# Both loops of a two-layer encoder kernel written out: no loop turns and no register arithmetic on any engine

## The chip, the cores and the metric

The kernel runs on one core of a Trainium2 chip. The metric is device time in microseconds (us) of one execution, from start to end of the program on that core. A core has five engines that matter here, each with a sequencer of its own that reads its own stream of instructions: TensorE (PE, matrix products; PEld is its weight load), VectorE (DVE), ScalarE (ACT), GpSimd (POOL) and SyncE (SP, which here issues all data transfers). They meet only at semaphores.

## The reference: what is computed

Two layers over a sequence of 1024 tokens with 1024 channels, in float32. Each layer modulates its input with a shift and a scale, mixes, multiplies with a gate, and normalises.

```python
for i in range(2):
    mod = silu(c) @ ada_w[i] + ada_b[i]
    shift, scale, gate = split(mod, 3)
    h = x * (1 + scale) + shift
    y = dilated_attention(h) if i == 0 else state_space(h)
    x = layer_norm(alpha * x + gate * y, ln_g[i], ln_b[i])
```

Layer 0 is attention with 16 heads of 64 channels and three dilations (1, 4, 16). For each dilation there are queries, keys and values; a query sees 128 keys around it, with a bias that falls with the distance. The three results are weighed by their softmax denominators, multiplied with silu of a gate projection, and projected.

Layer 1 is a bidirectional state-space mixer with 4 groups of 8 heads: a projection, a convolution over 5 tokens and silu, then for each direction a scan over 8 chunks of 128 tokens. A chunk contributes a masked product inside the chunk and a state of 128 x 512 that is carried, decayed, to the next chunk. The sum of both directions and a skip term is gated, normalised by its root mean square and projected.

## The kernel before

There is one hand-written program for each engine and each layer. Nothing is scheduled by a planner: the order of the work on an engine is the order in which the Python functions are called, and every dependency between engines is a semaphore with a count.

**Attention.** The projections run in units of two tiles (128 output channels each). Every unit is seven products of 12 matmuls (four blocks of the contraction, three terms of a high and a low float32 part), in a Strassen-like scheme: POOL and ACT make the seven weight forms (`low_part` L573 and around, `round_form`), PE multiplies (`product`, L688), DVE adds the seven products up in PSUM (`first_sums`, `second_sums`, L1317 to L1341). Between the units PE does the attention of the current head pair in ten "duos": `scores` (L742), `transpose_probs` (L752), `values` (L810, L821). DVE takes the row extremes (`tops`, L1282) and copies transposed probabilities (`copy_t`, L1302), ACT takes the exponentials (L1048) and copies projections and numerators (L987).

There are eight head pairs. Pairs 0 to 6 run in a loop with a register `j` on each engine; the eighth stands behind the loop as straight code (`last_pair` and its like) and does the same things in its first six duos. The five loops of the five engines are separate: PE's at L939, ACT's at L1177, POOL's at L649, SP's at L478, DVE's at L1537, and each engine turns around at its own place. DVE turns around just before the duo 1 of the next pair, behind the addition of L1330.

**State space.** Groups 0 to 2 run in a loop with a register `j` (PE L2535, ACT L2859, POOL L2296, SP L2173, DVE L3207), group 3 stands behind it as straight code with less and other work. What precedes group 0 is straight code as well. A group has eight chunk steps. In each one PE does six quarters of a projection unit for the next group (`project_k`, L2340), the state of a chunk (`state`, L2357), and `outputs` (L2372 and L2384). ACT opens the group with `conv_weights` (L2584 to `gconv`), the rounding of a weight tile (`split_hi`, L1970, to `w_hi_s`), `shift` (L2653), `back` (L2584 to `vv`), `centre` (L2593, L2595) and `exponentials` (L2660). POOL takes the low part of that tile (`split_lo`, L1960), then the inputs of the state (`decayed_inputs`, L2227, `xw`), and `weights` (L2240). DVE does `convolve` (L2970), `lesser` (L2898), `both` (L2906), `update` (L2917 to L2928). SP loads rows of factors (`load_rows` L2022, `load_ew` L2028) and weight tiles (`load_w` L1948). The last thing that ACT does in a group is `skip` of the fourth tile (L2584 to `trunk`), which waits for a transfer of SP (`send`, L2074) to be finished.

**How a loop is made.** In a loop every count that depends on `j` is worked out in registers by the engine's own sequencer, ahead of the instruction that waits for it, and so is every address that depends on `j` (`bass.ds(j, 1)`). At the end of the body stand an addition and a conditional branch.

```python
with act.Fori(0, GROUPS - 1) as j:
    group(j, False)
group(LAST, True)
```

Some helpers ask `isinstance(n, int)`: it tells a value known in Python (straight code) from a register (loop), and chooses a wait or a buffer by that.

Of the kernel before, what the change touches and what calls it, by code (L numbers as in the profile page):

```python
# [115 lines left out]
def attention_phase(nc, io, keep):  # L116
# [7 lines left out]
    with ExitStack() as ctx:  # L124
# [186 lines left out]
        def programs(block, after):  # L311
# [4 lines left out]
            def _(sp):  # L316
# [161 lines left out]
                with sp.Fori(0, PAIRS - 1) as j:  # L478
# [82 lines left out]
            def _(pool):  # L561
# [87 lines left out]
                with pool.Fori(0, PAIRS - 1) as j:  # L649
# [31 lines left out]
            def _(pe):  # L681
# [257 lines left out]
                with pe.Fori(0, PAIRS - 1) as j:  # L939
                    pair(j)  # L940
# [30 lines left out]
            def _(act):  # L971
# [205 lines left out]
                with act.Fori(0, PAIRS - 1) as j:  # L1177
# [91 lines left out]
            def _(dve):  # L1269
# [267 lines left out]
                with dve.Fori(0, PAIRS - 1) as j:  # L1537
# [172 lines left out]
def state_space_phase(nc, io, keep, first):  # L1710
    with ExitStack() as ctx:
# [131 lines left out]
        def x_place(n, i):  # L1843

            if isinstance(n, int) and i % 2:
                return yo_p[:, 0, :], yo_p[:, 1, 0:P]
            return fill[:], bt_p
# [78 lines left out]
        def paired(n, k):  # L1926

            return int(isinstance(n, int) and n == 0 and 0 < k < 7)
# [34 lines left out]
        def split_hi(act, n, slot):  # L1963
            act.wait_ge(w_in, 16 * n + 16)

            if not isinstance(n, int) or n > 3:
                wait(act, "pp_full", 2 * n - 2)
            elif n > 1:
                wait(act, "pp_full", n + 1)
# [47 lines left out]
        def programs(block):  # L2017
            @block.sync
            def _(sp):
                def load_rows(j, c):  # L2020
                    src = io["cum_rows"][c, :, bass.ds(j, 1)].rearrange("d a h t -> d (a h t)")
# [3 lines left out]
                def load_ew(j, c):  # L2025
                    for half in range(2):
                        src = io["exp_rows"][half, c, :, bass.ds(j, 1)].rearrange("d a k t -> d (a k t)")
# [3 lines left out]
                def load_fac(n):  # L2031
                    sp.dma_start(fac[:], io["fac"][bass.ds(n, 1)].rearrange("a p k -> p (a k)")
# [37 lines left out]
                def send(j, i):  # L2070
                    kt, hf_ = i // 2, i % 2
                    wait(sp, "y_gated", 8 * j + (i + 1))
                    dst = io["yT"][4 * hf_:4 * hf_ + 4, :, bass.ds(4 * j + kt, 1), :]
# [99 lines left out]
                with sp.Fori(0, GROUPS - 1) as j:  # L2173
                    group(j, False)
# [38 lines left out]
            def _(pool):  # L2213
# [82 lines left out]
                with pool.Fori(0, GROUPS - 1) as j:  # L2296
# [40 lines left out]
            def _(pe):  # L2337
# [51 lines left out]
                def unstage(n, i):  # L2389
                    if i == 0:  # L2390
                        wait(pe, "silu_done", UB * n + 10)
                    if not isinstance(n, int):
# [142 lines left out]
                with pe.Fori(0, GROUPS - 1) as j:  # L2535
# [46 lines left out]
            def _(act):  # L2582
# [18 lines left out]
                def tanh(tile, f, banked=False):  # L2601

                    wait(act, "pp_free", 3 if isinstance(tile, int) and tile == 0 else 2 * tile + 2)
# [17 lines left out]
                def conv_weights(g):  # L2621

                    src = conv[:, g, :] if isinstance(g, int) else conv[:, bass.ds(g, 1), :].rearrange(
                        "p a c -> p (a c)")
# [4 lines left out]
                def skip_weights(n):  # L2629
                    put(dg[:], dcol[:, bass.ds(4 * n, 4)]).then_inc(S["dg_set"], 1)  # L2630

                def skip(n, kt):
# [3 lines left out]
                    if not isinstance(n, int):  # L2636
# [222 lines left out]
                with act.Fori(0, GROUPS - 1) as j:  # L2859
# [35 lines left out]
            def _(dve):  # L2895
# [311 lines left out]
                with dve.Fori(0, GROUPS - 1) as j:  # L3207
# [137 lines left out]
```

## Time and profile before

| | |
|---|---|
| time of the kernel, three runs | 2128.47, 2129.84, 2132.52 us, median 2129.84 us |
| the execution that was profiled | 2126.8 us, of which the span of the instructions is 2124.7 us |
| mean granted clock of PE | 0.985 |
| attention loop, turns of the branch taken | 6 on each engine |
| state-space loop, turns of the branch taken | 2 on each engine |
| a pair of the attention loop | about 131 us |
| a group of the state-space loop | about 167 us |

The profile is a page of summaries, and views of the trace by line, by wait, by time, by window, and along the chain of work that ended last. In the views, "q" behind an engine (ACTq) is an instruction of its sequencer: register arithmetic, a branch, a semaphore, a transfer that it issues. "issue" is time in which an engine waited for nothing that the profile shows.

### The profile page before, as it was taken

How to read it: one execution, taken by the hardware profiler on the slowest of the kernel's cores; microseconds unless marked ns; L12 is line 12 of the kernel's file. 1: busy time of each engine (PE TensorE's matmuls, PEld its weight loads, DVE VectorE, ACT ScalarE, POOL GpSimd, SP SyncE). 2: the span in 40 equal slices, each digit the busy share in tenths (PEclk: the TensorE clock that was granted, in tenths of full speed). 3: DMA queues.
4: the chain of work that ended last, by engine and by line, in shares of the span. 5: the costliest groups of instructions: out<-in, count | busy, mean ns of one | idle time of the engine just before them, and what ended most of it. 6: DMA issues, size and time to landing. Idle time of an engine off the chain costs nothing.

```text
span 2124.7 us, 34188 instructions
## 1 busy us (share of the span) xinstructions
PE 1978.9 (93%) x10607; PEld 1569.4 (74%) x10607; DVE 1365.9 (64%) x2731; ACT 1052.8 (50%) x2574; POOL 1276.2 (60%) x845
## 2 busy tenths in 40 slices
PE   2689999999999999999997989899899899998997
PEld 1467777777777777777776868677687677777886
DVE  7745746557475564755646676797497498487553
ACT  3245455455445455544554254773574475584320
POOL 3456686775867758677583345475275366386572
PEclk9999999999999999999999999999999999999998
DMA  7312131221212222122224423464265265377431
GB/s 237 113 60 73 50 91 58 72 72 61 79 58 72 75 66 81 58 72 80 61 79 160 153 100 103 124 185 137 82 182 156 93 168 153 102 195 234 159 119 40
DMA packets 119606, 229.11 MB, mean 108 GB/s; under 512 B 22592, under 2 KB 65216, under 8 KB 119488
## 3 DMA queue, kind: packets, MB, share of 16 engines
q1 hardware_dynamic: 119488, 227.85, 34.7%
q8 instruction: 36, 0.59, 0.1%
q14 instruction: 82, 0.67, 0.1%
HBM read 199.42 MB, written 28.39 MB: 107 GB/s over the span
## 4 chain that ended last, share of the span: by engine, by line
PE 65%; DVE 14%; issue 8%; ACT 4%; POOL 4%; DMA 3%; SPq 1%; DVEq 0%; ACTq 0%; POOLq 0%
PE pp L688 24%; PE po L688 9%; PE pp_s L2340 7%; PE tp L752 3%; PE sp_ L742 3%; PE yo_p L2544 3%; DVE stage_s L2970 2%; DMA w_raw_s<-in_b_w 2%; PE pp_s L2544 2%; PE po L821 2%; DVE vv L2906 2%; PE st_p L2544 1%; PE po L810 1%; PE fill L2544 1%; PE tp L761 1%
## 5 line engine op out<-in xcount | busy, mean ns | idle before, releaser
L688 PE MATMUL pp<-h_forms_hi,w_f 128*128 128x512 f32 x1600 | 529.2, 400 | 42.2 <-DVE h_forms_lo L1438 31.9
L688 PEld LDWEIGHTS pp<-h_forms_hi,w_f 128*128 128x128 f32 x1600 | 304.0, 190 | 111.4 <-issue 42.0
L563 POOL TENSOR_TENSOR w_f<-w_raw,w_f 128x512 fp32r<-128x512 f32 x160 | 206.8, 1311 | 181.1 <-ACT w_f L987 181.1
L688 PE MATMUL pp<-h_forms_lo,w_f 128*128 128x512 f32 x800 | 314.3, 393 | 0.0
L2340 PE MATMUL pp_s<-h_hi,w_hi_s 128*128 128x512 f32 x624 | 270.5, 433 | 16.8 <-DVE stage_s L2970 9.6
L1048 ACT ACTIVATE prob<-prob,mz 128x256 f32<-128x256 f32 (+2 forms) x384 | 170.0, 444 | 231.6 <-DVE mz L1282 231.4
L2340 PE MATMUL pp_s<-h_hi,w_lo_s 128*128 128x512 f32 x624 | 246.3, 395 | 0.0
L2340 PE MATMUL pp_s<-h_lo,w_hi_s 128*128 128x512 f32 x624 | 246.0, 394 | 0.0
L688 PE MATMUL po<-h_forms_hi,w_f 128*128 128x512 f32 x640 | 214.9, 396 | 4.1 <-POOL w_f L563 4.1
L563 POOL TENSOR_TENSOR w_f<-w_f_raw,w_f 128x512 fp32r<-128x512 f32 x120 | 156.2, 1302 | 101.9 <-ACT w_f L987 101.9
L688 PEld LDWEIGHTS pp<-h_forms_lo,w_f 128*128 128x128 f32 x800 | 152.6, 191 | 29.1
L2340 PEld LDWEIGHTS pp_s<-h_hi,w_hi_s 128*128 128x128 f32 x624 | 118.5, 190 | 65.6 <-issue 35.1
L1302 DVE COPY probT<-tp 128x512 f32<-128x512 f32 x160 | 102.8, 683 | 89.2 <-PE tp L752 70.7
L1960 POOL TENSOR_TENSOR w_lo_s<-w_raw_s,w_hi_s 128x1024 fp32r<-128x1024 f32 x40 | 98.8, 2470 | 101.6 <-ACT w_hi_s L1970 101.6
L2970 DVE SCALAR_TENSOR_TENSOR stage_s<-pp_s,gconv,stage_s 128x512 f32<-128x512 f32 (+2 forms) x184 | 137.9, 750 | 20.4 <-ACT stage_s L2595 14.8
L688 PEld LDWEIGHTS po<-h_forms_hi,w_f 128*128 128x128 f32 x640 | 121.9, 190 | 30.9 <-POOL w_f L563 4.5
L2340 PEld LDWEIGHTS pp_s<-h_lo,w_hi_s 128*128 128x128 f32 x624 | 118.8, 190 | 31.0 <-issue 9.4
L2340 PEld LDWEIGHTS pp_s<-h_hi,w_lo_s 128*128 128x128 f32 x624 | 118.4, 190 | 26.5
L987 ACT ACTIVATE w_f<-w_f_raw 128x512 fp32r<-128x512 f32 x120 | 75.5, 630 | 121.7 <-POOL w_f_raw L608 90.4
L1282 DVE CUSTOM_DVE_ANT_0 prob<-sp_,bias,slope 128x256 f32<-128x256 f32 (+2 forms) x384 | 134.1, 405 | 2.1 <-DVE slope L1518 2.1
L2240 POOL TENSOR_TENSOR vv<-rw,vv 128x1024 f32<-128x1024 f32 x32 | 76.5, 2390 | 97.8 <-DVE vv L2906 81.6
L688 PE MATMUL po<-h_forms_lo,w_f 128*128 128x512 f32 x320 | 126.2, 394 | 0.0
(470 smaller groups left out, 4330.3 us busy)
## 6 DMA issues: line engine op xcount, KB each, us to landing
w_raw<-in_a_w SPq DMA_DIRECT2D x80, 512.0 KB, 3.2
rw<-cum_rows SPq DMA_DIRECT2D x32, 1024.0 KB, 6.2
w_raw_s<-in_b_w SPq DMA_DIRECT2D x40, 512.0 KB, 4.3
ew<-exp_rows SPq DMA_DIRECT2D x64, 256.0 KB, 7.2
qk<-merge_rows SPq DMA_DIRECT2D x42, 256.0 KB, 4.1
yT_b<-trunk SPq DMA_DIRECT2D x32, 256.0 KB, 2.3
v<-in_ada_w SPq DMA_DIRECT2D x40, 192.0 KB, 2.5
stage_s<-yT_b SPq DMA_DIRECT2D x15, 512.0 KB, 4.7
```

Source lines behind the costliest of these rows:

```text
L563: return nc.gpsimd.tensor_tensor(out, x, hi.bitcast(F32), ALU.subtract)
L688: last = nc.tensor.matmul(bank, w[:, b], h[:, b], start=b == 0 and t == 0, stop=b == KS - 1 and t == 2)
L742: last = nc.tensor.matmul(sp_[:, h, c:c + w], q[rows, P * n:P * n + P], kT[g][rows, k0:k0 + w], start=True, stop=True)
L987: return nc.scalar.activation(dst, src, ACT.Copy, **kw)
L1048: last = nc.scalar.activation(prob[:, u % 2, c:c + w], prob[:, u % 2, c:c + w], ACT.Exp, scale=-1.0, bias=mz[:, m:m + 1], accum_out=mz[:, ...
L1282: last = nc.vector.tensor_tensor_reduce(out=prob[:, u % 2, c:c + w], in0=sp_[:, u % 2, c:c + w], in1=bias[:, c0:c0 + w], scale=slope[:, h: ...
L1302: nc.vector.tensor_copy(dst, src).then_inc(t_free, 2 if ev[0] == "e" else 1)
L1960: nc.gpsimd.tensor_tensor(flat(w_lo[:, slot]), flat(w_raw[:]), flat(w_hi[:, slot]).bitcast(F32), ALU.subtract).then_inc(S["lo_done"], 1)
L2240: nc.gpsimd.tensor_tensor(flat(vv[:, c % 2]), flat(rw[:, c % 2, 1]), flat(vv[:, c % 2]), ALU.mult).then_inc(S["wx_done"], 1)
L2340: last = nc.tensor.matmul(out, w[:, slot, k, :], of_h(h, k, half), start=(k == 0 and n == 0), stop=(k == KT - 1 and n == 2))
L2544: ins = nc.tensor.matmul(acc(m, half), y, w[:, half * HALF:(half + 1) * HALF], start=(k == 0 and i == 0), stop=(k == KO - 1 and i == 2))
L2970: ins = nc.vector.scalar_tensor_tensor(out, src[:, a - 2 + k - half * HALF:b - 2 + k - half * HALF], w[:, k:k + 1], out, ALU.mult, ALU.add)
```

## The change

Every one of the ten loops becomes a Python loop, so that the program holds seven copies of a pair's code and three copies of a group's, with all counts and addresses as constants. The order of the working instructions on each engine is unchanged, and so are their number, their shapes and what they wait for. Since `j` is now always known in Python, the helpers' tests are put in terms of its value.

```diff
-                with sp.Fori(0, PAIRS - 1) as j:
+                for j in range(PAIRS - 1):
...
-                with pool.Fori(0, PAIRS - 1) as j:
+                for j in range(PAIRS - 1):
...
-                with pe.Fori(0, PAIRS - 1) as j:
+                for j in range(PAIRS - 1):
...
-                with act.Fori(0, PAIRS - 1) as j:
+                for j in range(PAIRS - 1):
...
-                with dve.Fori(0, PAIRS - 1) as j:
+                for j in range(PAIRS - 1):
...
-            if isinstance(n, int) and i % 2:
+            if n == 0 and i % 2:
...
-            if not isinstance(n, int) or n > 3:
+            if n > 3:
...
-                    src = io["cum_rows"][c, :, bass.ds(j, 1)].rearrange("d a h t -> d (a h t)")
+                    src = io["cum_rows"][c, :, j:j + 1].rearrange("d a h t -> d (a h t)")
...
-                    if not isinstance(n, int):
+                    if n:
                         wait(pe, "xu_free", 8 * n + i)
...
-                with sp.Fori(0, GROUPS - 1) as j:
+                for j in range(GROUPS - 1):
                     group(j, False)
                 group(LAST, True)
...
-                    src = conv[:, g, :] if isinstance(g, int) else conv[:, bass.ds(g, 1), :].rearrange(
-                        "p a c -> p (a c)")
+                    src = conv[:, g, :]
```

The loops of POOL, PE, ACT and DVE over the groups change as SP's does.

Three places, in the order in which instructions stand in the program (REGISTER_ALU and the bare ISA rows are register arithmetic).

ACT, end and beginning of the body of the loop over the groups, before; `trunk` is the output that `skip` begins, `gconv` holds the convolution's weights, `w_hi_s` the rounded weight tile, `rw` a chunk's rows:

```order
L2584 ACTIVATE trunk<-stage_s,dg 128x1024 x4
L2859 UNCONDITIONAL_BRANCH
L2859 ISA
L2584 ISA
L2584 ACTIVATE gconv<-conv 128x36
L1901 REGISTER_ALU
L1964 ISA
L1901 ISA
L1970 ACTIVATE w_hi_s<-w_raw_s 128x1024
L2651 ISA
...
L2859 REGISTER_ALU
L2859 COMPARE_AND_BRANCH
```

The same place now, at the entry of the first copy; the later copies read alike:

```order
L2584 ACTIVATE vv<-cbm,fac 128x128 x8
L2659 ACTIVATE rw<-rw,fac 128x128 x8
L2584 ACTIVATE trunk<-stage_s,dg 128x1024 x4
L2584 ACTIVATE gconv<-conv 128x36
L1970 ACTIVATE w_hi_s<-w_raw_s 128x1024
L2652 ACTIVATE rw<-rw,fac 128x128 x8
```

The five working instructions stand in the same order, with nothing between them.

DVE, end of the body of the loop over the pairs, before; `temps` and `pp` hold sums of the products, `probT` transposed probabilities:

```order
L1327 REGISTER_ALU
L1328 TENSOR_TENSOR temps<-pp,temps 128x512
L1329 REGISTER_ALU
L1330 TENSOR_TENSOR temps<-po,temps 128x512
L1537 REGISTER_ALU
L1537 COMPARE_AND_BRANCH
```

The end of the first copy and the beginning of the second, now:

```order
L1323 TENSOR_TENSOR pp<-pp,temps 128x512
L1328 TENSOR_TENSOR temps<-pp,temps 128x512
L1330 TENSOR_TENSOR temps<-po,temps 128x512
L1302 COPY probT<-tp 128x512 x2
L1282 ISA prob,mz<-sp_,bias,slope 128x256
```

The copy to `probT`, to which DVE had to branch back, follows the addition directly.

SP, the last chunk steps of a group of the state-space loop, before; `rw` and `ew` are rows of factors, `w_raw_s` is a weight tile:

```order
L1901 REGISTER_ALU
L2022 ISA
L2022 DMA rw<-cum_rows 128x2x1024
L1901 REGISTER_ALU
L2028 ISA
L2028 DMA ew<-exp_rows 64x2x512
L2028 ISA
L2028 DMA ew<-exp_rows 64x2x512
L1901 REGISTER_ALU
L1948 ISA
L1948 DMA w_raw_s<-in_b_w 128x1024
```

The same place now:

```order
L2022 DMA rw<-cum_rows 128x2x1024
L2028 DMA ew<-exp_rows 64x2x512 x2
L1948 DMA w_raw_s<-in_b_w 128x1024
```

The four transfers are in the same order, and the register arithmetic between them is gone.

## Rows read from the trace of the kernel before

**Rows 1.** The page: busy time of PE, and what was loaded on the instruction queues.

```profile
PE 1978.9 (93%) x10607; PEld 1569.4 (74%) x10607; DVE 1365.9 (64%) x2731; ACT 1052.8 (50%) x2574; POOL 1276.2 (60%) x845
...
q8 instruction: 36, 0.59, 0.1%
q14 instruction: 82, 0.67, 0.1%
```

**Rows 2.** Windows of attention: loop pairs 1 and 6, then the straight eighth; twice.

```profile
core 0: us, PE busy (x) PEld busy (x) DVE busy (x) ACT busy (x) POOL busy (x), PEclk, DMA share, GB/s
261.72:288.11 26.39, 25.68 (x149) 20.27 (x149) 13.47 (x34) 12.58 (x30) 21.19 (x15) 1.00 0.37 102
...
916.38:942.64 26.26, 25.68 (x150) 20.27 (x149) 13.48 (x34) 12.46 (x31) 21.04 (x15) 1.00 0.36 102
1047.23:1073.13 25.90, 25.66 (x150) 20.30 (x149) 13.56 (x34) 12.63 (x30) 20.76 (x14) 1.00 0.36 103
...
288.11:314.05 25.94, 25.94 (x157) 21.08 (x157) 12.43 (x33) 13.55 (x30) 23.10 (x16) 1.00 0.20 67
...
1073.13:1099.09 25.96, 25.96 (x158) 21.09 (x157) 12.45 (x33) 13.75 (x30) 23.50 (x17) 1.00 0.22 70
```

**Rows 3.** The chain, DVE's first turn (start us, us, what).

```profile
273.92 0.07 DVEq L1537
273.99 3.45 issue
277.44 0.07 DVEq L1537
```

**Rows 4.** PEld in time, where the next pair's values begin.

```profile
start us, us, engine line op out<-in xcount [idle before <-releaser]
284.92 0.85 PEld L821 LDWEIGHTS po<-probT,v 128*64 128x64 f32 x16 [1.08 <-ACT num L987]
```

**Rows 5.** Windows of the state space: two chunk steps in groups 0, 1 and 2.

```profile
1361.34:1387.89 26.55, 24.75 (x142) 19.54 (x141) 23.45 (x39) 22.87 (x70) 17.49 (x10) 1.00 0.60 175
1520.05:1554.82 34.77, 27.74 (x140) 21.00 (x140) 22.68 (x39) 25.13 (x75) 17.79 (x10) 0.85 0.42 132
1686.84:1721.73 34.89, 27.63 (x141) 21.03 (x141) 22.66 (x38) 25.13 (x75) 17.80 (x10) 0.85 0.44 130
1387.89:1449.40 61.51, 59.71 (x341) 47.73 (x340) 57.97 (x100) 42.75 (x126) 45.27 (x27) 1.00 0.58 161
1554.82:1616.29 61.47, 59.72 (x341) 47.73 (x340) 57.99 (x100) 42.90 (x126) 45.28 (x27) 1.00 0.59 161
```

**Rows 6.** ACT in time, its first turn from group 0 to group 1.

```profile
1518.66 1.15 ACT L2584 ACTIVATE trunk<-stage_s,dg 128x1024 f32<-128x1024 f32 x1 [1.10 <-DMA yT_b<-trunk]
1521.54 0.23 ACT L2584 ACTIVATE gconv<-conv 128x36 f32 x1 [1.73 <-issue]
1526.10 1.06 ACT L1970 ACTIVATE w_hi_s<-w_raw_s 128x1024 fp32r<-128x1024 f32 x1 [4.32 <-issue]
```

**Rows 7.** ACT in time, entry into group 0.

```profile
1355.60 3.22 ACT L2584 ACTIVATE trunk<-stage_s,dg 128x1024 f32<-128x1024 f32 x3
1358.73 0.21 ACT L2584 ACTIVATE gconv<-conv 128x36 f32 x1
1359.16 1.06 ACT L1970 ACTIVATE w_hi_s<-w_raw_s 128x1024 fp32r<-128x1024 f32 x1 [0.22 <-ACT gconv L2584]
```

**Rows 8.** POOL in time behind that turn, then PE in time.

```profile
1527.23 2.35 POOL L1960 TENSOR_TENSOR w_lo_s<-w_raw_s,w_hi_s 128x1024 fp32r<-128x1024 f32 x1 [7.24 <-ACT w_hi_s L1970]
1529.54 2.11 POOL L2227 TENSOR_TENSOR xw<-trunk,fac 128x512 f32<-128x512 f32 x1
...
1526.42 0.39 PE L2340 MATMUL pp_s<-h_hi,w_lo_s 128*128 128x512 f32 x1
1531.78 2.07 PE L2357 MATMUL st_p<-xw,bt 128*128 128x512 f32 x2 [4.97 <-POOL xw L2227]
1535.91 0.79 PE L2340 MATMUL pp_s<-h_hi,w_hi_s 128*128 128x512 f32 x1 [2.06 <-DVE stage_s L2970]
```

**Rows 9.** The chain at ACT's turn: the branch, and what follows it.

```profile
1518.74 0.04 ACTq L2859
1518.79 2.55 issue
1521.34 0.07 ACTq L2859
```

**Rows 10.** Window with the lower clock behind ACT's first turn.

```profile
1529.60:1539.80 10.20, 5.96 (x11) 3.62 (x12) 8.77 (x17) 10.20 (x35) 3.81 (x2) 0.50 0.15 51
```

**Rows 11.** Chain, end of a group: SP's queue between POOL and a weight tile; PE.

```profile
1616.28 0.02 issue
...
1618.72 8.40 DMA w_raw_s<-in_b_w
...
1635.05 0.49 PE L2340 MATMUL pp_s<-h_hi,w_hi_s 128*128 128x512 f32 x1 [1.44 <-DVE trunk L3151]
```

**Rows 12.** SP in time, the same transfers in group 3, which is straight code.

```profile
1863.14 0.37 SPq L2022 DMA_DIRECT2D rw<-cum_rows  x1
1863.56 1.32 SPq L2028 DMA_DIRECT2D ew<-exp_rows  x2
1864.92 0.78 SPq L2152 DMA_DIRECT2D hb<-hb_s  x1
```

**Rows 13.** The queues of stretches 100:255 and 260:1040: packets, MB, share of 16 engines.

```profile
q8 instruction: 7, 0.11, 0.3%
q14 instruction: 7, 0.06, 0.1%
...
q14 instruction: 31, 0.25, 0.1%
```

More of the change, by code:

```diff
@@ L1926, in paired @@
         def paired(n, k):
-            return int(isinstance(n, int) and n == 0 and 0 < k < 7)
+            return int(n == 0 and 0 < k < 7)
         def xw_of(n, k):
@@ L2026, in load_ew @@
                     for half in range(2):
-                        src = io["exp_rows"][half, c, :, bass.ds(j, 1)].rearrange("d a k t -> d (a k t)")
+                        src = io["exp_rows"][half, c, :, j:j + 1].rearrange("d a k t -> d (a k t)")
                         sp.dma_start(ew[HD * half:HD * half + HD, c % 2],
@@ L2031, in load_fac @@
                 def load_fac(n):
-                    sp.dma_start(fac[:], io["fac"][bass.ds(n, 1)].rearrange("a p k -> p (a k)")
+                    sp.dma_start(fac[:], io["fac"][n:n + 1].rearrange("a p k -> p (a k)")
                                  ).then_inc(fac_in, 16)
@@ L2072, in send @@
                     wait(sp, "y_gated", 8 * j + (i + 1))
-                    dst = io["yT"][4 * hf_:4 * hf_ + 4, :, bass.ds(4 * j + kt, 1), :]
+                    dst = io["yT"][4 * hf_:4 * hf_ + 4, :, 4 * j + kt:4 * j + kt + 1, :]
                     sp.dma_start(dst.rearrange("m p a t -> p m (a t)"),
@@ L2295, in group @@
                     weights(j + 1, 0)
-                with pool.Fori(0, GROUPS - 1) as j:
+                for j in range(GROUPS - 1):
                     group(j, False)
@@ L2534, in group @@
                             products(j + 1, i // 4)
-                with pe.Fori(0, GROUPS - 1) as j:
+                for j in range(GROUPS - 1):
                     group(j, False)
@@ L2601, in tanh @@
                 def tanh(tile, f, banked=False):
-                    wait(act, "pp_free", 3 if isinstance(tile, int) and tile == 0 else 2 * tile + 2)
+                    wait(act, "pp_free", 3 if tile == 0 else 2 * tile + 2)
                     wait(act, "silu_done", 2 * tile)
@@ L2629, in skip_weights @@
                 def skip_weights(n):
-                    put(dg[:], dcol[:, bass.ds(4 * n, 4)]).then_inc(S["dg_set"], 1)
+                    put(dg[:], dcol[:, 4 * n:4 * n + 4]).then_inc(S["dg_set"], 1)
                 def skip(n, kt):
@@ L2635, in skip @@
                     wait(act, "silu_done", UB * n + (2 * kt + 2))
-                    if not isinstance(n, int):
+                    if n:
                         act.wait_ge(y_out[kt], 32 * n)
@@ L2857, in _ @@
                 SQ_READ = [n + 1 if c == 0 else m + 1 for n, (m, c) in enumerate(ORDER)]
-                with act.Fori(0, GROUPS - 1) as j:
+                for j in range(GROUPS - 1):
                     group(j, False)
@@ L3205, in normalise @@
                                             ALU.mult).then_inc(normed, 1)
-                with dve.Fori(0, GROUPS - 1) as j:
+                for j in range(GROUPS - 1):
                     group(j, False)
```

## The prediction

> **What bounds the kernel now.** I read the page first: PE is busy for 1978.9 of 2124.7 us [rows 1], so almost everything that saves time must let PE start something sooner. DVE, ACT and POOL are busy for 64, 50 and 60% and matter only where PE waits for them. Then I looked for places where a loop's body can be set beside straight code that does the same work, since the change turns the one into the other. Windows of both loops give that [rows 2, 5]. Last I followed the chain and the engines in time around each turn of a loop [rows 3, 4, 6 to 9], the clock behind it [rows 10], the queue of SP [rows 11, 12] and the queues that carry instructions [rows 13].
>
> **Register arithmetic on PE: nothing.** The change takes some thousand register instructions from PE's sequencer. Does PE wait for them? The stretch from duo 2 to duo 4 lasts 25.94 us inside the loop and 25.96 us in the eighth pair, which is straight code with constants [rows 2]. PE is busy throughout in both. So this part is costed at 0. The cover is PE's own work: the arithmetic is done while matmuls are queued, and the equal windows show that it suffices.
>
> **Turns of the attention loop: 2.7 us.** There are six taken turns on each engine. On DVE the branch is followed by 3.45 us in which nothing runs and nothing is waited for [rows 3]. That delays the row extremes of the next duo, then ACT's exponentials and copies, and some ten microseconds later PE stands 1.08 us before the values of the next duo [rows 4]. The window that holds this, duo 0 to duo 2, shows the price: 26.39 us at the first turn, 26.26 at the sixth (26.46, 26.35, 26.36 and 26.24 at those between), against 25.90 in the straight pair, at the same PE busy time of 25.7 [rows 2]. The differences are 0.49, 0.56, 0.45, 0.46, 0.34 and 0.36, together 2.66 us. Most of DVE's 3.45 us is hidden by PE's queue of matmuls. The lower end is 6 x 0.2 = 1.2 us, if a part of the difference is due to the eighth pair's other tiles; the upper end is PE's whole wait, 6 x 1.08 = 6.5 us. I take 2.7, since the window measures PE itself. The turns of the other engines in this loop show no wait on PE and count nothing.
>
> **Turns of the state-space loop: 16.2 us.** Two turns are taken. ACT finishes `skip`, starts `gconv` 1.73 us after it could and the rounding of the weight tile 4.32 us after `gconv`, with no releaser for either [rows 6]. From the start of the last `skip` to the rounding it is 1526.10 - 1518.66 = 7.44 us. At the entry to group 0, which has no turn, the last of the three merged `skip`s starts about 1.05 us before `gconv` at 1358.73, and the rounding comes at 1359.16: 1.48 us [rows 7]. So ACT loses 5.96 us at each turn. Who waits for that: POOL sat 7.24 us before the low part of this tile, and only behind that does it make `xw`; PE waits 4.97 us for `xw`, then 2.06 us for DVE's convolution, which hangs on ACT through the rows [rows 8]. Without the loss POOL ends `xw` at 1531.65 - 5.96 = 1525.7, before PE is through with its matmuls at 1526.65, so the first wait goes. The second wait ends 5.96 us sooner, at 1529.95 in place of 1535.91. PE would reach it about 1.1 us after 1526.65, so 2.2 us of waiting stay there: DVE and ACT are late next. There is a second gain. After the turn PE's granted clock is 0.50, its level of 1.2 GHz, for 10.2 us [rows 10], behind PE's wait of 4.97 us. In the 3.9 us of that stretch in which products run, a matmul of 512 columns takes 0.43 us where it takes 0.23 us elsewhere: ten of them lose 2.0 us. A wait of 2.2 us may or may not lower the clock; group 0 has one of 1.8 us at the same granted clock of 1.00, so I count the 2.0 as gained. Sum of this working: 5.96 + 2.0 = 8.0 us a turn.
>
> The windows give the same in another way. Two chunk steps last 34.77 and 34.89 us behind the turns and 26.55 us in group 0, which is entered without one; the five steps that follow last 61.51 and 61.47 us, alike [rows 5]. The differences are 8.22 and 8.34 us. I take 8.1 a turn, 16.2 for both. Lower end: PE's first wait alone, 4.97 us each, 9.9 in all. Upper end: both waits and the clock, 4.97 + 2.06 + 2.0, 18.1 in all.
>
> **Register arithmetic on the other engines: 1.5 us.** Inside the five equal steps PE is idle for 61.5 - 59.7 = 1.8 us [rows 5], and nothing says that arithmetic is the cause; I take 0, at most 3 x 1.8 = 5.4. At the end of a group a weight tile is late: from POOL's end at 1616.28 to the start of its transfer at 1618.72 SP spends 2.44 us on three other transfers and the arithmetic before each, and the tile's rounding delays what PE waits 1.44 us for [rows 11]. In straight code the same three take 1864.92 - 1863.14 = 1.78 us [rows 12], and I add 0.15 for the waits: 0.5 us sooner, in three groups, 1.5 us. Lower end 0, upper end 3 x 1.44 = 4.3 us.
>
> **Streaming of instructions: 0.** What is added is code to be fetched. Queue 8 carries 36 blocks of instructions in the whole span [rows 1], none in the 780 us of attention loop after its first pass, and 7 in the 155 us around and in that first pass [rows 13]. At that rate, 7 in 155 us, the loops' later passes (790 us of attention, 360 of state space) need about 52 blocks more. PE's price for them is read from straight code: the eighth pair fetches its code, and its steps are as long as the loop's [rows 2]. On the other queue the loops already fetch, 31 blocks in those 780 us [rows 13], so little is added. I take 0; a gain is excluded, the loss is a rival below.
>
> **What the Trainium skill says.** The trace shows 2.55 us between ACT's branch and its next instruction, while the branch itself is 0.04 us [rows 9]. The Trainium skill, "Runtime: NRT & Kernel Launch", section on instruction fetch mechanics, says that fetching is sequential and that a taken branch out of the pages held forces a fetch before the engine can go on; the trace agrees for ACT and DVE. It also says that crossing into a next page of straight code is mostly hidden, which the equal windows bear out.
>
> **The sum.** 2.7 + 16.2 + 1.5 = 20.4 us, from the profiled 2126.8 us: 2106.4 us. That execution was 3.04 us faster than the median of 2129.84 us, so on the median I predict **2109.4 us**, 0.96% less.
>
> **The rivals.** *Half of it in the state space.* ACT's delay goes, but another link takes its place: DVE turns around at the same time, and POOL has three things to do before PE's second wait ends. Then only PE's first wait goes (9.9 us), with 1.2 to 2.7 from attention: 11 to 13 us, about 2118 us. Against it, group 0 has all these links and takes 26.55 us. *More than that.* The arithmetic also holds up the chain between DVE, ACT, POOL and SP inside a group: with the upper ends 6.5 + 18.1 + 4.3 + 5.4 it is 34 us, about 2096; half of the excess gives 2102. For it, the chain has a lot of "issue" in the state space; against it, PE is 97% busy in the equal steps. *The turns cost only the branch.* What follows a branch would have been a wait for something else. The branch of 0.04 us [rows 9] on the deciding engine, eight times, is 0.3 us, and the time stays at 2129.5 us. Against it, the entry to group 0 runs the same instructions without the delay [rows 7].
>
> The "Advanced Engine Details and Errata" page of the Trainium skill, section on control flow timing, gives about 108 ns for a compare-and-branch; by that figure eight turns would be an estimate of 0.9 us, and the time would not measurably change. The trace shows 0.04 us for the instruction, and 2.55 us until the next.
>
> *Slower: PE's code arrives late.* PE's loops now run without fetching. If each of the 52 added blocks held PE up, by as much as a branch holds ACT (2.55 us), the loss would be 133 us; the gain of 20.4 us is used up at 0.4 us a block, and from there the kernel is slower. With 1 us a block it is 2109.4 + 52 = 2161 us. It would be likeliest in the state space, where transfers are busy for 0.58 of the time [rows 5]. Against it stand the windows of the straight pair.
>
> **How the numbers follow.** The forecast, about 2109, has 0.62. Half of it, about 2118, has 0.17. More, about 2100, has 0.12. The turns cost only the branch: 0.05. Slower: 0.04. The range is to leave out no more than the last two and the farthest parts of "more": 2101 to 2119. About 0.2%, 4 us, is what a measurement of this kernel can tell from no change. Faster by more than that is the first three cases, 0.91; no change 0.05; slower 0.04.
>
> **What would show it.** In the profile after: DVE's copy to `probT` follows its addition without the 3.45 us; the windows from duo 0 to duo 2 last 25.9 us in all pairs; ACT's rounding starts about 1.5 us after the last `skip`; the windows of two chunk steps last about 26.6 us in all three groups, at a granted clock of 1.00; queue 8 has some 85 to 90 blocks instead of 36, without a PE wait at them. The prediction is wrong if the two chunk steps stay above 30 us, or if PE shows new idle time of about a microsecond every twenty.

## The result, and the profile after

The straight kernel takes 2112.07 us (median of 4 runs, 2110.16 to 2117.66) against 2129.15 us beside it (2127.25 to 2132.52): a ratio of 0.9919, 95% interval 0.9902 to 0.9936. That is 17 us faster; predicted were 20.4 us and 2109.4. A second comparison gave 2113.77 against 2130.31, ratio 0.9923 (0.991 to 0.9937). The first profiled execution of the straight kernel took 2117.66 us (span 2115.8), 5.6 above its median, while that of before, 2126.8, lay 2.3 below its own. So the two traces differ by 8.9 us only, and below I use a second profile of the straight kernel too (run e10, span 2114.0, 10.7 us below before).

The page of after, the rows that answer to [rows 1]. As predicted, queue 8 carries 50 blocks more; queue 14 carries fewer, since the loops had fetched their bodies again at every turn.

```profile
PE 1976.5 (93%) x10607; PEld 1570.4 (74%) x10607; DVE 1369.5 (65%) x2731; ACT 1054.0 (50%) x2574; POOL 1278.1 (60%) x845
q8 instruction: 86, 1.41, 0.3%
q14 instruction: 63, 0.52, 0.1%
```

Three stretches by windows: up to the state space, its groups 0 to 2, the rest. First before, then after (columns as in [rows 2]). In this pair of executions the whole gain is in the second stretch, 11.4 us, and the attention part gained nothing. The second profile says the same: 1364.7, 477.5 and 271.8 us, so 15.1 us less in the groups and 3.4 us more in what precedes them. What the medians gain beyond that, some 6 us, stands in no trace.

```profile
0.00:1361.34 1361.34, 1268.70 (x6999) 1006.08 (x6999) 841.00 (x1823) 652.09 (x1551) 850.66 (x584) 0.99 0.28 88
1361.34:1853.87 492.53, 463.13 (x2407) 363.22 (x2407) 358.26 (x684) 291.59 (x784) 264.66 (x157) 0.98 0.48 140
1853.87:2124.70 270.83, 247.10 (x1202) 200.16 (x1202) 166.62 (x224) 109.15 (x242) 160.86 (x106) 0.97 0.47 151
```

```profile
0.00:1363.05 1363.05, 1268.89 (x7000) 1006.90 (x7000) 843.36 (x1823) 653.67 (x1552) 851.09 (x584) 0.99 0.29 88
1363.05:1844.16 481.11, 459.90 (x2407) 362.48 (x2407) 359.58 (x684) 291.28 (x784) 264.71 (x157) 0.99 0.50 143
1844.16:2115.80 271.64, 247.74 (x1202) 201.06 (x1202) 166.59 (x224) 109.09 (x241) 162.28 (x106) 0.97 0.47 150
```

Windows of attention after, duo 0 to duo 2 in pairs 1, 2, 5, 6 and the eighth, as in [rows 2]. Pairs 2, 3, 4 and the eighth take 25.7 us, even less than the 25.9 that I expected. Pairs 1, 5 and 6 take longer than inside the loop (26.39, 26.24 and 26.26): something new waits there.

```profile
262.52:290.73 28.21, 25.73 (x151) 20.30 (x150) 15.87 (x34) 12.65 (x30) 21.79 (x15) 1.00 0.35 93
395.32:421.05 25.73, 25.49 (x151) 20.31 (x150) 13.39 (x34) 12.68 (x30) 20.57 (x15) 1.00 0.38 103
...
786.22:812.76 26.54, 25.70 (x151) 20.30 (x150) 14.21 (x34) 12.67 (x30) 20.87 (x15) 1.00 0.36 100
917.32:944.16 26.84, 25.69 (x151) 20.30 (x150) 14.57 (x33) 12.76 (x30) 21.51 (x15) 1.00 0.34 99
1048.72:1074.45 25.73, 25.49 (x152) 20.31 (x150) 13.39 (x34) 12.68 (x30) 20.57 (x15) 1.00 0.38 102
```

Windows of the state space after, two chunk steps in groups 0, 1 and 2, as in [rows 5]. The 34.8 and 34.9 us of groups 1 and 2 are 28.9 and 27.3, the clock is back at 0.94 to 1.00. Group 0 has lost 1.3 us in this execution, at a clock of 0.94; in the second profile it takes 26.3 us at 1.00, so that loss does not belong to the code.

```profile
1363.05:1390.89 27.84, 26.06 (x141) 20.72 (x140) 24.87 (x41) 22.60 (x69) 17.42 (x10) 0.94 0.65 186
1522.05:1550.90 28.85, 26.36 (x140) 20.66 (x141) 23.98 (x41) 23.59 (x72) 17.50 (x10) 0.94 0.58 180
1683.98:1711.24 27.26, 24.77 (x140) 19.51 (x141) 22.59 (x39) 23.61 (x72) 17.51 (x10) 1.00 0.59 170
```

ACT in time at the same place as [rows 6]. Behind the last `skip` the rounding of the weight tile starts after 1.30 us instead of 7.44, with no idle time at all.

```profile
1519.30 1.15 ACT L2584 ACTIVATE trunk<-stage_s,dg 128x1024 f32<-128x1024 f32 x1
1520.35 0.22 ACT L2584 ACTIVATE gconv<-conv 128x36 f32<-128x36 f32 x1
1520.60 1.06 ACT L1970 ACTIVATE w_hi_s<-w_raw_s 128x1024 fp32r<-128x1024 f32 x1
```

### The profile page after: what moved, and what is told of

It is laid out like the page before. It is cut to its first block, busy times and chain, and to the rows that moved or that the text cites. A ratio compares the mean times of both kernels' runs of the same rounds, so it can differ in the third digit from the quotient of the medians.

```text
span 2115.8 us, 30206 instructions
## 1 busy us (share of the span) xinstructions
PE 1976.5 (93%) x10607; PEld 1570.4 (74%) x10607; DVE 1369.5 (65%) x2731; ACT 1054.0 (50%) x2574; POOL 1278.1 (60%) x845
## 4 chain that ended last, share of the span: by engine, by line
PE 67%; DVE 9%; POOL 8%; issue 7%; ACT 5%; DMA 3%; SPq 1%; POOLq 0%; DVEq 0%; ACTq 0%
PE pp L688 25%; PE po L688 9%; PE pp_s L2340 7%; PE tp L752 4%; PE sp_ L742 4%; PE yo_p L2544 3%; DMA w_raw_s<-in_b_w 3%; PE po L821 2%; POOL trunk L2249 2%; PE pp_s L2544 2%; POOL vv L2240 2%; PE po L810 2%; PE st_p L2544 1%; PE fill L2544 1%; POOL w_lo_s L1960 1%
## 5 line engine op out<-in xcount | busy, mean ns | idle before, releaser
L2969 DVE SCALAR_TENSOR_TENSOR stage_s<-pp_s,gconv,stage_s 128x512 f32<-128x512 f32 (+2 forms) x184 | 137.9, 750 | 20.6 <-ACT stage_s L2595 15.1
L2340 PEld LDWEIGHTS pp_s<-h_lo,w_hi_s 128*128 128x128 f32 x624 | 118.6, 190 | 30.9 <-issue 9.4
L2340 PEld LDWEIGHTS pp_s<-h_hi,w_lo_s 128*128 128x128 f32 x624 | 118.1, 189 | 26.6
```

What stands on the lines that cost most here:

```text
L2340: last = nc.tensor.matmul(out, w[:, slot, k, :], of_h(h, k, half), start=(k == 0 and n == 0), stop=(k == KT - 1 and n == 2))
L2969: ins = nc.vector.scalar_tensor_tensor(out, src[:, a - 2 + k - half * HALF:b - 2 + k - half * HALF], w[:, k:k + 1], out, ALU.mult, ALU.add)
```

## The experiments

In all kernels the loops are made by one generator, so that each engine and each loop can be chosen alone: `for j in turns(act, GROUPS - 1, how)`. With nothing said an engine keeps its loop. "Windows" are those of the two chunk steps of groups 1 and 2 (before: 34.8 and 34.9 us) and those from duo 0 to duo 2 (before: 26.2 to 26.5 us). Runs e1 to e4 were compared with 2129.08 us, e5 to e8 with 2131.18, e9 to e11 with 2130.31, e12 with 2130.52.

**Which loop.**

```
-for j in turns(every engine, GROUPS - 1, "loop")
+for j in turns(every engine, GROUPS - 1, "out")
```

> Only the five loops over the groups of the state space are written out; the loops over the head pairs stay. If the gain is ACT's and DVE's turns there, this run keeps most of it: 12 to 16 us under the kernel before, about 2115 us, and two chunk steps behind a turn last 27 to 29 us instead of 34.8. If the gain is spread over both loops by the register arithmetic, it keeps about a third to a half: 6 to 9 us.

2119.76 us, ratio 0.996 (0.9947 to 0.9973). That is 9.3 us, less than the 12 to 16 of the first theory and at the edge of what the second expected. The windows decide for the first: they fall to 29.4 and 28.9 us, 11.4 us in all. The attention, which stays a loop, has longer windows in pairs 5 and 6 (27.4 and 27.9), which eats a part.

```
-for j in turns(every engine, PAIRS - 1, "loop")
+for j in turns(every engine, PAIRS - 1, "out")
```

> Only the five loops over the head pairs are written out. By the windows of the straight eighth pair this gives 2.7 us (0.4 us for each of DVE's six turns). In the profile of the changed kernel three of the seven pairs had a new wait of 0.8 to 2.4 us for POOL's weight form, so 0 to 4 us is open. A theory in which arithmetic on PE costs time in the pairs expects more than 6 us here, since most of the arithmetic is in these loops.

2118.66 us, ratio 0.9946 (0.9933 to 0.9959): 10.4 us, where I had expected 4 at most and the theory of costly arithmetic more than 6. The windows of attention are 25.7 us in pairs 2 to 5, 25.9 in pair 6, and 26.6 and 26.5 in pairs 1 and 8. But the state space, whose loop is untouched, is faster too:

```profile
1522.58:1553.52 30.94, 27.45 (x141) 21.61 (x141) 23.35 (x40) 25.14 (x75) 17.80 (x10) 0.89 0.50 153
1685.34:1715.97 30.63, 26.52 (x141) 20.56 (x141) 22.72 (x39) 25.15 (x75) 17.81 (x10) 0.94 0.48 150
```

ACT in time shows why. The stall of 1.75 us behind the branch is there as before, but the one of 4.32 us before the rounding [rows 6] is gone. The loop is the same code; only its place in ACT's program has moved. The two windows are 8.1 us shorter by it, which leaves about 2 us of the 10.4 for the attention, so the theory of costly arithmetic is not borne out. For the same reason the gains of this kernel and the one before it can't be added up.

```profile
1523.66 0.23 ACT L2608 ACTIVATE gconv<-conv 128x36 f32 x1 [1.75 <-issue]
1524.12 1.06 ACT L1994 ACTIVATE w_hi_s<-w_raw_s 128x1024 fp32r<-128x1024 f32 x1 [0.22 <-ACT gconv L2608]
```

**Turn or arithmetic.** Straight copies in which the index still stands in a register, so that the register arithmetic stays and no branch is taken (each copy is a loop of one turn, which ends in a branch that falls through):

```
+for i in range(n):
+    with eng.Fori(i, i + 1):
+        regs_mov(regs, i)
+        yield snap(regs, min_val=0, max_val=n - 1)
```

> All ten loops are written out, but each copy gets its index in a register, so that all the register arithmetic of the loops is still done (979 additions and multiplications on PE, 1258 on DVE, as before) while no branch is taken back. If the turns cost the time, it is as fast as the changed kernel, within 3 us (16 to 18 us under the kernel before, less the 1.5 us that I gave to the arithmetic). If the arithmetic does, it is as slow as the kernel before.

2116.31 us, ratio 0.9941 (0.9927 to 0.9954). So the turns are worth about three quarters of the gain or more. By the medians the arithmetic is worth the rest, 2.5 to 4 us (2116.31 against 2113.77 and 2112.07), but the intervals of the ratios overlap, and these copies also hold more code (89 and 90 blocks on queues 8 and 14, where the straight kernel has 86 and 63). Windows of attention, pairs 1 and 2:

```profile
262.08:288.11 26.03, 25.67 (x152) 20.27 (x150) 13.57 (x34) 12.85 (x30) 20.70 (x15) 1.00 0.37 102
392.67:418.70 26.03, 25.68 (x151) 20.27 (x150) 13.56 (x34) 12.86 (x30) 20.88 (x15) 1.00 0.37 102
```

26.35 with turns, 26.03 with arithmetic alone, 25.70 with neither: in a pair each is worth about 0.3 us. Here no pair is slower than 26.11 us; the waits of pairs 1, 5 and 6 are not there.

**Branch or fetch.** Loops on all engines, as before, with the program's hint at the branch that it goes back:

```
-with Fori(0, n) as j:
+with Fori(0, n, 1, hint_back_edge=True) as j:
```

> The loops, the arithmetic and the turns of the kernel before stay as they are; each engine is only told at the top of every turn that the branch at the end will be taken, so that it can fetch the code for it ahead. If the time behind a branch is that of fetching the loop's first instructions, the stalls of 2.6 to 4.3 us on ACT and 3.5 us on DVE go and the time is near the changed kernel's, 2110 to 2116 us. If it is the branch itself or the emptied queue, the stalls stay and the time is 2129 us.

2120.91 us, ratio 0.9952 (0.9938 to 0.9966): half of the straight kernel's gain, and 5 us above the range that I had expected. The branches are all still taken; the stalls are gone. Windows of attention are 26.04 us in every pair. At ACT's turn (the chain, then the page's row of the queue):

```profile
1518.62 0.05 ACTq L120
1518.67 0.17 issue
1518.84 0.03 ACTq L120
```

```profile
q14 instruction: 33, 0.27, 0.0%
```

0.17 us in place of 2.55 [rows 9], and 33 blocks in place of 82. So it was never the branch that cost, but fetching the body again. Nor is the code fetched ahead, as I had thought: queue 14 carries no block at all between 208 and 1088 us, and none between 1443 and 1883 us. Why a hinted body stays at hand is not shown. The hint is an instruction more on each engine, and the place of a body matters, as the next runs show; but the stalls of DVE's six turns and of ACT's two all went at once. The hinted loop has one stall that no other profile shows, 3.54 us of DVE in group 3 at 1904.60, beside a fetch on queue 14; it makes the last stretch 4 us longer.

**Where the body starts.** The chain of before, right behind [rows 9]:

```profile
1521.44 0.05 ACTq L2584
1521.49 0.05 issue
1521.54 0.23 ACT gconv L2584
1521.77 4.05 issue
```

ACT gets its block after 2.55 us, runs three instructions of it, and stands again. My reading was that the body starts three instructions ahead of the end of a block. I moved it by eight instructions and changed no other instruction of the program:

```
+for _ in range(16):               # two waits make one instruction
+    act.wait_ge(row_full, 1)      # long past
 for j in turns(act, GROUPS - 1, "loop"):
```

> The kernel before with all its loops, and eight more instructions on ACT (waits for an event long past) ahead of its state-space loop, so that the loop's body starts eight instructions further on in ACT's program. In the trace of before ACT comes to its body's start after 2.6 us, runs three instructions and stands 4.3 us more. If that second stall is there because the body starts three instructions ahead of the end of a fetched block, it goes: two chunk steps of groups 1 and 2 fall from 34.8 to about 30.9 us (the value of the kernel with straight pairs, where it was not seen either), and the time by 2 x 3.9 = about 8 us, to 2121. Rival: a loop of this size always stands twice; then the windows stay at 34.8 us and the time within 1 us of before.

2118.51 us, ratio 0.9936 (0.9923 to 0.9949). Both expectations fell short: not only the second stall went, the first one too. The chain at ACT's turn, then the windows:

```profile
1520.87 0.04 ACTq L121
1520.91 0.22 issue
1521.13 0.07 ACTq L121
```

```profile
1522.41:1551.05 28.64, 24.79 (x140) 19.56 (x141) 22.71 (x39) 24.92 (x74) 17.75 (x10) 1.00 0.54 159
1683.98:1713.43 29.45, 26.35 (x141) 20.69 (x141) 24.13 (x41) 24.14 (x74) 17.73 (x10) 0.94 0.57 167
```

Moved by 32 instructions instead (`range(64)`):

> As the kernel with ACT's state-space body eight instructions further on (12.7 us faster than before, and no stall over 0.5 us at ACT's turns), but 32 instructions further on. Theory A: ACT keeps a small number of fetched blocks, and the body stays in them only where it starts close behind the start of a block; 32 further on it reaches into one block more, so the stall of 2.6 us behind the taken branch is back (and DVE's 3.2), while the second, 4.3 us, stays away, since the next block's end is far: two chunk steps 30 to 31 us, as in the kernel with straight pairs (30.9, 30.7), about 2122 to 2124. Theory B: only the end of a block right behind the body's start does harm; then it stays as with eight: windows 28 to 29 us, 2117 to 2120.

2123.89 us, ratio 0.9965 (0.9952 to 0.9979). Theory A held: the first stall is back, the second is not (the same two views).

```profile
1519.54 0.04 ACTq L121
1519.58 2.51 issue
1522.10 0.07 ACTq L121
```

```profile
1521.65:1553.10 31.45, 26.61 (x141) 20.54 (x140) 24.13 (x41) 25.27 (x75) 17.74 (x10) 0.95 0.55 160
1685.05:1715.55 30.50, 27.09 (x140) 21.30 (x141) 22.98 (x39) 25.14 (x75) 17.79 (x10) 0.89 0.51 152
```

From one turn to the next ACT runs 374 instructions. A block on queue 14 holds about 128 (an estimate: the straight kernel's 63 blocks for some 8150 instructions of ACT, DVE, GpSimd and SP). If the body starts three ahead of a block's end it touches four blocks, eight further on (the fifth of a block) three, and 32 further on (the 29th) four again. ACT's attention loop, 268 instructions, turns in 0.20 to 0.22 us everywhere. The explanation that a body in three blocks is still at hand and one in four is not fits the three positions; it does not explain the hint, and how many blocks an engine keeps I did not measure.

The Trainium skill, "Runtime: NRT & Kernel Launch", section on instruction fetch mechanics, says that a taken branch whose target lies outside the pages held has to wait for a fetch. These runs bear that out: 0.22 us with the body at one place, 2.51 us twenty-four instructions further on.

Something else moved that I had not touched. In e5, e9 and e8 (below) queue 8 carries 45 blocks instead of 36, though PE keeps its loops. In each of them one of PE's two turns in the state space takes 5.07, 5.09 and 4.72 us instead of 0.22, with nine blocks more behind it, and PE stands 1.25, 1.40 and 0.90 us (PE in time, e5):

```profile
1676.51 0.49 PE L2368 MATMUL pp_s<-h_hi,w_hi_s 128*128 128x512 f32 x1 [1.25 <-issue]
```

So PE's loops can be fetched again too; why they were in these three kernels and not in the others no run shows.

**Which engine.**

```
-for j in turns(act, GROUPS - 1, "loop")
+for j in turns(act, GROUPS - 1, "out")
```

> The state-space loop written out on ACT alone; the four other engines and the attention stay loops. Theory of the prediction: ACT's stalls (2.6 + 4.3 us at each turn) are those that PE feels, DVE's 3.2 us lie beside ACT's rounding of the weights. Then nearly all of the state-space gain is here: two chunk steps fall from 34.8 to 27 to 29 us, the time by 12 to 15 us, to about 2115. Rival: DVE's stall, or the sum of several engines, holds PE; then less than half comes, 2121 or more.

2117.71 us, ratio 0.9936 (0.9924 to 0.9948); windows 28.2 and 28.7 us. The complement, all engines but ACT straight in this loop:

> The complement of the run before: the state-space loop written out on SP, GpSimd, PE and DVE, a loop on ACT alone. Theory: the windows of two chunk steps stay within 1 us of 34.8 and the time within 2 us of before (2127 to 2130). Rival (others' stalls held PE too): 4 us or more of gain.

2126.32 us, ratio 0.9977 (0.9968 to 0.9985); windows 30.9 and 31.5 us. That is 4.9 us of gain, where I expected 2 at most and the rival, others' stalls hold PE too, 4 or more. ACT's second stall is shorter in it, 1.90 us before the rounding instead of 4.32. In the loops ACT's and DVE's blocks are fetched one right behind the other at the turn (at 1519.19 and 1519.66 us in before); with DVE straight only ACT's is (at 1525.5 us). So the stalls that PE feels are mainly ACT's, and it may be that DVE's fetch lengthens one of them; I did not test this by itself.

```
-for j in turns(dve, PAIRS - 1, "loop")
+for j in turns(dve, PAIRS - 1, "out")
```

> The attention loop written out on DVE alone. Theory: the whole attention gain sits on DVE, its stall behind the taken branch and its register arithmetic: the stretch from the second to the fourth scores of a pair falls from 26.3 - 26.4 to about 25.75 us, 0.6 us in each of six pairs, 3.6 us in all. A part of the kernel with all pairs straight (10.4 us faster) also came from the shifted state-space body on ACT, and that does not move here: 2125 to 2126. Rival: the gain needs ACT's or GpSimd's copy too; then within 1 us of before.

2126.56 us, ratio 0.9982 (0.9973 to 0.9991): 4.6 us by the medians and 3.8 by the ratio, as expected. The windows of attention are 25.84 to 25.90 us in all seven pairs, those of the state space stay at 34.9 and 34.4.

**PE's streamed code.**

```
-for j in turns(pe, ..., "loop")
+for j in turns(pe, ..., "out")
```

> Both loops written out on PE alone: 50 more blocks of PE's instructions are streamed (queue 8 some 86 instead of 36) and its register arithmetic goes; the other engines keep their loops. The prediction put both at nothing, its slower rival was code that comes late to PE. Theory: within 2 us of before, and no PE gap that two neighbouring instructions don't explain. Rival: every block costs PE 0.1 us or more; then 5 us slower, and the straight kernel's gain was cut by as much.

2138.57 us against 2130.31, ratio 1.0039 (1.0026 to 1.0051): **8.3 us slower**. The theory fell. Queue 8 carries 86 blocks, and PE's waits without a releaser are those of before (one, 1.2 us). What is longer are the windows of attention, all but pair 2's by 0.3 us or more, and those of groups 0 and 1 (28.1 and 35.6 us, before 26.6 and 34.8). Three of attention, pairs 1, 3 and 6 (26.39, 26.35 and 26.26 before):

```profile
261.71:289.02 27.31, 25.69 (x152) 20.31 (x150) 14.48 (x33) 12.70 (x31) 21.87 (x16) 1.00 0.38 99
...
524.72:552.18 27.46, 25.65 (x151) 20.30 (x150) 13.57 (x34) 13.33 (x31) 22.05 (x16) 1.00 0.36 98
...
919.61:949.52 29.91, 27.27 (x151) 21.50 (x150) 15.78 (x34) 13.24 (x31) 23.00 (x17) 0.94 0.32 90
```

**Pairs 1, 5 and 6 again.** The changed kernel a second time:

> The changed kernel once more, for a second profile and in one comparison with the others: 17 us faster than before (2112). In its first profile PE waited 2.5, 0.8 and 1.1 us in the second scores of pairs 1, 5 and 6, for a transfer of the running sums that landed late. If that belongs to the code, the same pairs wait again; if it is a matter of the execution, other pairs do or none, the six pairs take 130.3 us each and the profiled run is 3 to 4 us shorter.

2113.77 us. The same three pairs wait again, 26.54, 26.58 and 29.78 us, and no others: it belongs to the code. SP in time in the first profile, pair 1 and pair 2, shows where it begins:

```profile
250.59 3.90 SPq L331 DMA_DIRECT2D stats<-st  x8
...
383.39 2.79 SPq L331 DMA_DIRECT2D stats<-st  x8
```

The eight stores of the running sums take 3.90 us to issue instead of 2.79, since one of them takes 1.38 us instead of 0.33. From 250.58 to 251.92 us a block of PE's code is under way. I counted 98 of these places in all 14 profiles (seven sets of stores in each). With no block under way (29 places) the longest issue is 0.32 to 0.35 us; with one on queue 14 alone (46) it is 0.36 to 0.87; with one on queue 8 alone (13) it is 0.33 to 0.35 seven times and 0.94 to 1.45 six times; with both (10) it is 0.34 to 1.34. So a block goes with a long issue, but not always, and in the eighth set, behind the loop, one issue takes 0.54 us in e3 with no block under way. A late store makes the sums come back late, and what follows on DVE multiplies it. DVE in time, pair 1 and pair 2 of after:

```profile
258.99 0.27 DVE L1353 TENSOR_TENSOR cm<-cz 32x64 f32<-32x64 f32 x1 [1.70 <-DMA cz<-stats]
...
262.73 1.22 DVE L1363 TENSOR_TENSOR cm<-cz 32x64 f32<-32x64 f32 x1
263.98 1.22 DVE L1364 TENSOR_TENSOR cm<-cm,cz 32x64 f32<-32x64 f32 x1
...
395.62 0.21 DVE L1363 TENSOR_TENSOR cm<-cz 32x64 f32<-32x64 f32 x1
395.86 0.21 DVE L1364 TENSOR_TENSOR cm<-cm,cz 32x64 f32<-32x64 f32 x1
```

The same two operations take 1.22 us each, where GpSimd is adding at that moment, and 0.21 us each where it is not. Over all 14 profiles these two take 0.21 to 0.22 us at each of the 177 places where GpSimd adds nothing, and up to 1.35 us where it does. ACT, then GpSimd's `w_f` and PE follow (GpSimd and PE in time):

```profile
271.89 1.27 POOL L563 TENSOR_TENSOR w_f<-w_f_raw,w_f 128x512 fp32r<-128x512 f32 x1 [4.92 <-ACT w_f L987]
...
273.21 0.50 PE L688 MATMUL pp<-h_forms_hi,w_f 128*128 128x512 f32 x1 [2.25 <-POOL w_f L563]
```

This chain does not explain all of e11. In its pairs 3 and 4 the nine stores take 3.2 and 3.3 us (before 3.6 and 3.2), the longest issue is 0.38 and 0.44 us, and the merge of the sums ends as long after the first store as before, yet the windows are 1.1 and 0.8 us longer. There DVE's stall at its turn is longer (3.74 and 3.73 us, before 3.40 and 3.41), and PE waits 1.8 and 1.4 us for ACT's numerators instead of 0.6. So PE's code delays more than one thing.

To test the chain I moved the blocks of PE's code against the stores:

```
 pair_sums(0)
+for _ in range(60):
+    pe.wait_ge(ones_set, 1)       # long past; 30 instructions
```

> The changed kernel with 30 more instructions on PE (waits for an event long past) at 16 us of the span, where PE waits 9 us anyway, so that each block of PE's code is fetched 30 instructions earlier. In both profiles of the changed kernel PE waited in the second scores of pairs 1, 5 and 6 and nowhere else; in these pairs a block of code (queue 8 in pairs 1 and 6, queue 14 in pair 5) was under way while SP issued the nine stores of the running sums, and one of those issues took 0.6 to 1.45 us instead of 0.33. Theory: the block delays the issue, the sums come back late, DVE's small operations fall beside GpSimd's, and PE waits up to 4 us. By the times of the blocks, moved by 30 instructions no queue-8 block meets the stores in any pair: pairs 1 and 6 fall to 130.3 us (from 131.1 to 132.8 and 131.4 to 134.4), pair 5 stays at 131.1, and the median to 2109 or 2110, 3 us below the changed kernel's. Rival: the waits belong to something else in pairs 1 and 6; then they stay, and the time is 2112 to 2114.

2112.06 us, ratio 0.9911 (0.9897 to 0.9925), profiled span 2109.4. Against the second comparison of the straight kernel that is 1.7 us by the medians, too little to be told apart, and the 2109 to 2110 that I had expected did not come; the time is the rival's. The blocks moved by 0.8 us in pair 1 and 1.5 us in pair 6, not by 5: I had taken PE's records for its instructions. So pair 6's block still meets the stores, now earlier, and costs less (window 26.66 us, after 26.84 and 29.78). Pair 1's block ends as they begin: the longest issue is 0.34 us, yet its window is 26.54, as in the second profile. So the late issue is not all of pair 1's wait, and this test does not show the chain to be the cause. There the sums came 0.58 us late, and a block on queue 14 is under way at that moment; which block or engine does it, I leave open. In pair 5, too, the block on queue 14 stayed and the window is 26.51.

## Why the prediction was right, and where it was not

The median, 2112.1, is 2.7 us above the predicted 2109.4, and the mechanism of the large term is shown. That the sum came so close is luck in part: the three small terms were each off, and the gain predicted for attention, 2.7 us, is in neither profile, where the stretch up to the state space is 1.7 and 3.4 us longer.

**Register arithmetic on PE, 0.** Right for the window it rested on: from duo 2 to duo 4 the straight pair 2 takes 25.95 us, as before (25.94). But this window shows PE's part alone. In the same pairs the arithmetic was worth 0.3 us (26.03 against 25.7), about half of it DVE's (25.86 with DVE straight alone), and I had no term for that in attention: six pairs, 2 us. The straight eighth pair of before could not show it, since it came behind loop pairs and took 25.90; in the straight kernel it takes 25.73.

**Turns of the attention loop, 2.7.** The turn alone is 0.3 us a pair, 2 us, by the kernel with arithmetic and no turns. How most of DVE's 3.45 us is hidden can be read more sharply than I did: at all six turns of before the window less DVE's stall (3.28 to 3.52 us) is 22.94 to 22.96 us. With no stall it is 26.03, so about 3.1 us of a stall are hidden, and each microsecond beyond costs PE one. Turn and arithmetic together give 0.65 us in an undisturbed pair, 3.9 in six. In the first profile pairs 1, 5 and 6 gave 1.8 + 0.3 + 0.6 us back, in the second 0.2 + 0.3 + 3.5.

**Turns of the state-space loop, 16.2.** The mechanism is shown: ACT alone straight brings the windows to 28.2 and 28.7 us, and a shift of ACT's body by eight instructions to 28.6 and 29.5. The size was a little high. The windows fell by 5.9 and 7.6 us, in the second profile by 7.5 and 7.6, where I had 8.1 each. They don't reach the 26.55 of group 0: both have PE's wait of 1.80 us for DVE's convolution, but groups 1 and 2 have 0.69 us for the same one step earlier and 0.9 us for GpSimd's `vv` besides. That 0.69 is what is left of the second wait, where I had worked out 2.2 (and PE's matmuls end at 1526.81 us by [rows 8], not at 1526.65). Over the three groups the stretch is 11.4 us shorter, in the second profile 15.1 (492.5 to 477.5). "DVE and ACT are late next" was the right warning, and too little was charged for it. The clock came back in the second profile, 1.00 in all three groups. In the first it was 0.94 in groups 0 and 1 and 1.00 in group 2, with the same waits of PE in groups 1 and 2 (2.5 and 0.9 us); what made the difference is open.

**Register arithmetic elsewhere, 1.5.** SP's queue got shorter as worked out, but that was worth nothing in the two profiles. Three transfers in front of the weight tile now take 1.79 us, as forecast, but the tile's own transfer takes 10.76 us in place of 8.40 [rows 11], and PE's wait at the group's end stays, 1.6 us in both (1.4 before).

```profile
1611.85 0.38 SPq L2022
...
1613.62 10.76 DMA w_raw_s<-in_b_w
```

**Streaming of instructions, 0.** This step failed. The number of blocks was right (50 more, 52 worked out), but I read their price from the straight eighth pair, where none was paid. PE straight alone is 8.3 us slower, 0.17 us for each of its 50 blocks on average. The price is not paid at PE's own fetch. A part of it goes with late issues on SP and DVE's chain behind them, in pairs 1 and 6 above all; the rest, as in pairs 3 and 4 of e11, is not explained. In the straight kernel a part of it remains in pairs 1, 5 and 6. The rival with a loss by late code looked for it at PE's own fetch; the loss is real, and its place was another. Together with ACT's and DVE's straight code the loss stayed well below the gain.

**The rivals.** "Only PE's first wait goes" is out: the windows fell by 5.9 to 7.6 us, and of PE's second wait, 2.06 us, 0.69 is left. "Only the branch" is out by the hinted loops. "More than that" got little: inside a group the five equal steps are 60.8 and 61.1 us against 61.5.

## What to carry to other kernels

A loop whose body is fetched again at a turn paid 2.5 us for it on ACT and 3.3 to 3.5 us on DVE, and ACT paid 4.05 us once more where its body started just ahead of a block's end. Look for idle time with no releaser right behind a branch, on an engine that PE depends on; here writing the loop out on that engine alone, or moving its body by eight instructions, gave three quarters of the gain (2117.7 and 2118.5 us). How much of a stall reaches PE has to be read from the window behind it: on ACT nearly all of it did, on DVE only what went beyond 3.1 us. Writing out the busiest engine's loops, which showed no stall, cost 50 blocks of code and 8.3 us.

## What was unexpected of the hardware

- The same loop on ACT costs 2.55 + 4.05 us at its turn, 2.51 us, or 0.22 us, by where its body starts (as it was, 32 and 8 instructions further on).
- A hint at the backward branch removes these stalls with the loop kept: 0.17 us, and 33 blocks on queue 14 instead of 82; the bodies are then not fetched again at all.
- PE's loops were not fetched again at their turns in the kernel before (36 blocks on queue 8 in the whole span), ACT's in the state space and DVE's were. In three other kernels (e5, e8, e9) PE's was once, with a branch of 4.7 to 5.1 us.
- With a block of code under way the longest of SP's nine issues of stores is up to 1.45 us (above 0.35 us at 61 of 69 places); without one it is 0.32 to 0.35 us at 29 places.
- A DVE operation on 32x64 elements takes 0.21 us alone and 1.22 us beside an addition on GpSimd.
